# Paired expert rows thinned over the dense phase, their three steps a block apart, the weight split ahead of the dot

## The reference

```python
q = einsum(xb, w_q)                        # 8 heads, 2 halves of 128
s = einsum(q, keys)                        # 128 scores per half
s_top, i_top = top_k(s, 16)                # per half
cand = s_top[0][:, None] + s_top[1][None]  # 256 candidates
best, sel = top_k(cand, 16)
eidx = cand_idx[sel]                       # 16 of 16384 experts per head
gate = softmax(best)
act = gelu(einsum('td,thkd->thk', xb, u_tab[eidx]))
coef = gate * act
h += einsum('thk,thkd->td', coef, v_tab[eidx])
```

## Time and profile before

| | |
|---|---|
| time, median of 3 runs | 2142.16 us (2139.93 to 2144.28) |
| the profiled execution's own time | 2143.07 us |
| its span in the trace | 2141.0 us |
| mean granted TensorE clock | 0.972 of full |
| busy shares | PE 90%, PE weight load 73%, DVE 63%, ACT 29%, POOL 32% |

### The profile page before, as it was taken

One profiled execution on the slowest core, in us unless ns is written; L12 is line 12 of the kernel. 1 busy time (PEld: TensorE's weight loads), 2 busy tenths in 40 slices (PEclk: granted clock), 3 DMA queues, 4 the chain that ended last, 5 costly groups with the idle time before them and its releaser, 6 DMA issues.

```text
span 2141.0 us, 29757 instructions
## 1 busy us (share of the span) xinstructions
PE 1934.9 (90%) x10912; PEld 1564.2 (73%) x10912; DVE 1358.9 (63%) x2860; ACT 616.4 (29%) x1217; POOL 675.5 (32%) x556
## 2 busy tenths in 40 slices
PE   5998889988996988999999999998899998999886
PEld 4997889978966988998999999998544433434332
DVE  3219263353345535488988888988377777776663
ACT  4223312252224324444445444445300000000000
POOL 0003012100000000232333233232277776776663
PEclk9999899988998999999999999999999999999999
DMA  3557158637614573899999999999499999999997
GB/s 117 197 198 220 31 180 260 216 86 257 237 41 178 177 261 119 318 366 349 403 388 361 388 394 357 376 364 376 184 412 403 404 407 412 397 398 415 405 414 290
DMA packets 244650, 629.25 MB, mean 294 GB/s; under 512 B 19714, under 2 KB 137541, under 8 KB 226712
## 3 DMA queue, kind: packets, MB, share of 16 engines
q0 software_dynamic: 74880, 377.52, 44.5%
q1 hardware_dynamic: 169632, 249.92, 34.4%
HBM read 584.36 MB, written 110.21 MB: 324 GB/s over the span
## 4 chain that ended last, share of the span: by engine, by line
DMA 19%; PE 15%; DVE 14%; issue 7%; ACT 2%; POOL 2%; SPq 1%; DVEq 1%; another core or an unknown queue 0%; ACTq 0%; POOLq 0%
DMA ex_w_raw<-in_peer_ut 10%; DMA ex_uv_row<-value_rows,ex_eidx 9%; PE ps L2137 9%; DVE ex_fin L2388 4%; DVE ex_w_lo L1935 3%; POOL ex_uv_row L2066 2%; PE ps L589 2%; PE ps L590 2%; PE ps L591 2%; DVE ex_uv_row L2376 2%; ACT ex_w_hi L2199 1%; DVE ex_q_s L2401 1%; DVE ex_top_i L2335 0%; SPq L1989 0%; DVEq L162 0%
## 5 line engine op out<-in xcount | busy, mean ns | idle before, releaser
L2137 PE MATMUL ps<-ex_uv_row,ex_q_s 128*128 128x512 f32 (+1 forms) x1208 | 542.4, 599 | 61.3 <-DVE ex_q_s L2401 47.3
L2137 PEld LDWEIGHTS ps<-ex_uv_row,ex_q_s 128*128 128x128 f32 (+1 forms) x1208 | 217.1, 187 | 366.3 <-issue 347.6
L2066 POOL DMA_INDIRECT ex_uv_row<-value_rows,ex_eidx x384 | 405.2, 1055 | 214.6 <-issue 102.2
L589 PE MATMUL ps<-x_hi,ex_w_lo 128*128 128x384 f32 (+2 forms) x1296 | 427.6, 330 | 27.8 <-DVE ex_w_lo L1935 22.6
L590 PE MATMUL ps<-x_lo,ex_w_hi 128*128 128x384 f32 (+2 forms) x1296 | 423.6, 327 | 0.0
L591 PE MATMUL ps<-x_hi,ex_w_hi 128*128 128x384 f32 (+2 forms) x1296 | 423.5, 327 | 0.0
L2050 POOL DMA_INDIRECT ex_uv_row<-in_peer_uv,ex_eidx x128 | 190.6, 1489 | 410.2 <-DVE ex_fin L2388 404.7
L2388 DVE SCALAR_TENSOR_TENSOR ex_fin<-ex_uv_row,ret_tables,ex_fin 128x1024 f32<-128x1024 f32 x218 | 278.7, 1279 | 0.3
L589 PEld LDWEIGHTS ps<-x_hi,ex_w_lo 128*128 128x128 f32 x1296 | 244.6, 189 | 40.7 <-DVE ex_w_lo L1935 30.7
L591 PEld LDWEIGHTS ps<-x_hi,ex_w_hi 128*128 128x128 f32 x1296 | 245.0, 189 | 0.0
L590 PEld LDWEIGHTS ps<-x_lo,ex_w_hi 128*128 128x128 f32 x1296 | 244.8, 189 | 0.0
(11 more groups left out here) (415 smaller groups left out, 3418.5 us busy)
## 6 DMA issues: line engine op xcount, KB each, us to landing
value_rows<-in_peer_uv SPq DMA_DIRECT2D x64, 1024.0 KB
ex_w_raw<-in_peer_ut SPq DMA_DIRECT2D x128, 512.0 KB
value_rows<-ex_z_rows SPq DMA_DIRECT2D x128, 128.0 KB
first_raw<-in_w_in SPq DMA_DIRECT2D x8, 1024.0 KB, 7.9
ex_w_raw<-in_peer_wq SPq DMA_DIRECT2D x16, 512.0 KB
value_rows<-ex_z_rows SPq DMA_DIRECT2D x128, 64.0 KB
dp_w_raw<-in_w_in SPq DMA_DIRECT2D x14, 512.0 KB
ex_uv_row<-value_rows,ex_eidx POOLq DMA_INDIRECT x384
```

Of the source, the lines that this page charges most:

```text
L589: pe.matmul(out, left(llo, c), right(rhi, c), start=(c == 0), stop=False)
L2066: pool.indirect_dma_start(value_slot(p)[0], None, k.value_rows, bass.IndirectOffsetOnAxis(ap=eidx[:, u, n % TOPK:n % TOPK + 1], axis=0), e ...
L2137: ins = pe.matmul(k.pv[j % 2][0:r, c, :], spread[:, on_tensor[p] % SPREADS, 0:r], v[:, c * 512:(c + 1) * 512], start=first, stop=last)
```

## The change

Which block a row is taken at now comes from a table, `row_at`: rows begin at block 6 instead of 8, and no row is taken at blocks 16, 32, ... 128. That leaves 130 rows (`beside`) beside the loop; the last six stand behind it. On DVE `lower(i + 2)` comes ahead of `dot`. ACT takes `row` one row later than DVE's `dot`, and the sum (`add_vector`, and `add_row` on PE) two rows later than the dot. The condition in PE's loop asks for a row above 129, which no block has, so all eight sample rows are summed behind PE's loop. Nothing is left out of the computation and the order of the sums is the same.

```diff
-ROWS_FROM = 8
+ROWS_FROM = 6
...
+    row_at = dict(zip((i for i in range(ROWS_FROM, len(blocks)) if i % TOPK), range(PAIRS)))
+    beside = len(row_at)
...   PE
-                    if HK <= i - ROWS_FROM - 1 < PAIRS:
-                        add_row(i - ROWS_FROM - 1)
-                for p in range(len(blocks) - ROWS_FROM - 1, PAIRS):
+                    if row_at.get(i, 0) > HK + 1:
+                        add_row(row_at[i] - 2)
+                for p in range(max(HK, beside - 2), PAIRS):
                     add_row(p)
...   ACT
-                    if 0 <= i - ROWS_FROM < PAIRS:
-                        row(i - ROWS_FROM)
+                    if row_at.get(i, 0) > 0:
+                        row(row_at[i] - 1)
...
-                for p in range(len(blocks) - ROWS_FROM, PAIRS):
+                for p in range(beside - 1, PAIRS):
                     row(p)
...   DVE
-                    p = i - ROWS_FROM
-                    if 0 <= p < PAIRS:
-                        dot(p)
+                    p = row_at.get(i, -1)
                     if 5 <= i + 2 < len(blocks) and by_dve(i + 2):
                         lower(dve, i + 2)
-                    if 0 < p <= HK:
-                        add_vector(p - 1)
-                    if p == HK:
+                    if p >= 0:
+                        dot(p)
+                    if 1 < p <= HK + 1:
+                        add_vector(p - 2)
+                    if p == HK + 1:
                         add(0)
...
-                for p in range(len(blocks) - ROWS_FROM, PAIRS):
+                for p in range(beside, PAIRS):
                     dot(p)
+                    if p <= HK + 1:
+                        add_vector(p - 2)
+                    if p == HK + 1:
+                        add(0)
```

## The result

The changed kernel took 2126.64 us (median of 20 runs, 2122.09 to 2131.91), the kernel before 2141.51 beside it (20 runs, 2124.12 to 2148.48): a ratio of 0.9932, 95% interval 0.9918 to 0.9946. It is faster by 14.9 us, inside the range of 2100 to 2133, and by little more than half of the 27 us forecast. The 95% interval of a ratio is given in brackets from here on. The profiled execution took 2126.57 us, its span is 2124.5.

The account below looks back on a forecast made before the run. PE, DVE and DMA were all near their limit in the dense phase, with some 36 us of PE stalls from late loads. Stalls 20 plus loop end 7 make 27 us off, so 2115 us, range 2100 to 2133.

Parts of the forecast that it names:

- The stalls: Dense phase: of some 36 us of PE stalls, 20 us go, with the loop ending at about 1499.
- the reading: Dense phase: a self-feeding loop, DVE's late dot delaying ACT, the store, the next load and DVE again.
- The wait for the dot: ACT in the dense phase: its wait for DVE's dot falls from 140.8 to under 20 us.
- I count nothing: DVE's order, `lower` ahead of the dot: no gain or loss, since DVE's cycle is the same either way.
- The slower rival: Dot exposed behind DVE's wait for `w_hi`: +37 us, less 20 and 7, about 2152; chance 0.05.
- The rate: DMA in the dense phase: 226.7 MB to move by the loop's end, going above 374 GB/s (378).
- The end of the loop: From PE's last dense block to the first value row: 7 us gained, 5.8 plus 1 for PE's clock.
- Gain 5.8: Loop's end: first value row at 1536.6 instead of 1542.42, before any stall is saved; between 4 and 7.7 us.
- the terms of row 135: Last row behind the loop: gather issued at T + 2.1, landed T + 10, dot ended T + 11.2, value row about T + 17.3.
- The value gathers: Loop's end: last store in at about T + 3.6, value gathers from T + 4, their 6.8 us hidden under sample rows.
- The value phase: After the dense phase: fed by DMA at a share of 1.01, it moves as a whole.
- The limit of bandwidth: HBM at about 358 GB/s per core would need 633 us, leaving a gain near zero; the trace disagreed.

Follow-up runs that it names:

- the stagger alone: Kernel before with only the distances changed: activation one row and sum two rows behind the dot; 0.9932 of the kernel before.
- the thinning alone: Kernel before with only the `row_at` table: rows from block 6, none at blocks 16, 32, ... 128; 0.9921 of the kernel before.
- the order alone: Kernel before with only `lower` put ahead of the dot on DVE; 1.0269 of the kernel before, 57 us slower.
- the kernel without empty blocks and with the dot first: Changed kernel with a row in every block from 6 to 141 and the dot ahead of `lower`; 0.9964 of the kernel before, median 2129.55 us.
- the change with the dot first: Changed kernel with the dot ahead of `lower` again, as in the kernel before; 0.9905 of the kernel before.
- the kernel with small last gathers: Changed kernel with the gathers of rows 133 to 135 fetching 8 floats per partition instead of 2048; 0.9911 of the kernel before.
- the filler: Changed kernel with two unneeded DVE sums over `x_first` added in each of the eight empty blocks; 0.9945 of the kernel before.
- the kernel with rows from block 4: Changed kernel with rows from block 4, dot ahead of `lower`, sample rows 128 and 129 summed in PE's loop; 0.9895 of the kernel before, median 2120.52 us.

## Why the prediction was half right

**The stalls: right in size, the reading borne out in part.** An end of the loop near 1499 was forecast, with 20 us of stalls gone; measured 1500.8 and 17.9. PE's wait for `w_lo` fell from 22.6 to 11.6 us (about 10 forecast). That ACT's wait for the dot delayed the store, and the store the next load, fits the stagger alone, which is 15 us faster. But there PE still waits 16.7 us, and with the thinning alone ACT waits 121.2 us for the dot and PE only 9.8. So this link is one way to the stalls and not the only one. The stagger alone and the thinning alone each bring as much as the whole change (0.9932 and 0.9921 against 0.9932), in their profiles 9 and 16 us of the dense phase, and together 18: for the most part they take away the same stalls.

**The wait for the dot: less than said.** It fell to 44.9 us, not under 20. With the dot ahead of `lower` it is 24.4, in the stagger alone 14.8. The step that failed here is that of `lower`, "I count nothing". The cycle of DVE is indeed the same in either order, but the ring that matters also runs through ACT. The slower rival had the place right (the dot behind the wait for `w_hi`), gave +37 us by DVE's load, and the order alone costs 57 by another mechanism: a ring of 4.44 us at the least and 5.2 or more where DVE has a part of `retrieve`. In the change the stagger opens that ring; by the middles (0.9932 against 0.9905) the order still costs some 6 us there, which the intervals don't set apart from nothing.

**The rate: wrong in sign.** DMA was to go above 374 GB/s; it is 371, with 1.00 for the share. The prediction's bytes had one gather behind the loop's end; three were issued there. So by 1500 the loop had moved 371 x 600 us = 222.6 MB from 900 on, not 226.7, and did not need a faster queue. That a faster one can be had the kernel without empty blocks and with the dot first shows, at 376 GB/s over the same window. That kernel and the change with the dot first (0.9964 and 0.9905) stand apart, so the thinning is worth something beside a stagger from block 6; against the stagger alone (0.9932) that is not shown. In three of the changed kernel's units of 16 blocks, 48 to 96, block to block takes 70.89 us, which is 14 x 4.21 and 2 x 5.78 within 0.4: hardly a stall is left there. What remains stands mostly at both ends of the phase, and the two largest stalls lie behind the loads that SP issues after its series of small DMAs.

**The end of the loop: the step that failed by size and sign.** "Gain 5.8", plus 1 for the clock: 7. Measured: T to V grew by 12.3 us, all that the six moved rows had freed, and V to the end by 1.9; the gain is -2. The error is in the terms of row 135. Its gather was issued at T + 5.1, not T + 2.1: PE began row 128, whose slot it needs, only at T + 1.6, since ACT formed that row's factors late, behind the `z_rows` of block 142 (1501.04), and when PE was done at T + 3.5, POOL was still at the issue of row 134's gather, until T + 4.8. Then 11.1 us passed from issue to dot, not 7.9. Together that is 6.2 us, and V came at T + 23.3 instead of T + 17.3. From the dot on the chain was right: 7.1 us measured, 7.3 forecast. The value gathers went wrong as well: the first started at T + 17.1, not T + 4, because the store ahead of it took 13.7 us and was in at T + 16.3, where the sum had it in at T + 3.6. But it had landed (1522.32) 1.3 us before DVE was free for the first `picked` (1523.60), so this second error lay beside the first and not on top of it. That the kernel with small last gathers has V at T + 16.8, close to the 17.3 of the prediction, is in part luck: its row 135 was issued late too and landed in time because it was small. The steps named were the true ones; what was missing is the price of three gathers, the last store and POOL's own issues at the same time.

That the total came out inside the range is owed to the stalls. Of 27 us, 20 were to come from them and 18 did; 7 were to come from the end and 2 were lost there.

**The value phase**: 598 to 601 us in every kernel, so it moves as a whole, as said.

**The limit of bandwidth.** The Trainium skill (DMA: Bandwidth & Descriptors, Specifications) gives 358 GB/s for one core, and works it out as half of 716 for two cores. The changed kernel, one core alone, ran at 371 over 600 us and 405 over 570 us, so that half is no ceiling for it, and the measurement decides again.

**Open.** Whether the order of `lower` costs anything in the full change (0.9932 and 0.9941 against 0.9905) is not settled, nor whether the filler costs the last few us, nor whether an empty block helps by its missing gather or by ACT's free time. No run moved SP's two series of small DMAs, and none shortened the last gathers alone or the last store alone. Which of the store's companions delays it most, the three gathers or the 512 KB load of the norm's weights between the stores (10.1 us to landing, 3.7 before), was not tried apart.

## What to carry to other kernels

When an engine waits inside its own queue, write the order of each engine out as one ring and add up a turn: a ring through two engines that both have idle time can be slower than the engine that you look at, and a step back by one block opens it. Add up the longest turn too: a ring without reserve passes on every extra piece of work. When two edits remove the same stall, do not add them; take each alone. And work that is moved out of a loop must be priced with the transfers it then runs beside. List every path that the next phase waits for (here the last gather by way of dot and norm, and the last store by way of the first value gather), and check in the trace which one ended last: the engine that starts without idle time is on it.

## What the hardware did that I had not expected

The last store of `z_rows`, 64 KB, took 13.7 us beside three gathers of 1 MB, 7.3 in the kernel with rows from block 4, 5.1 beside the small gathers, and 1.8 in the kernel before, where no gather ran. Over 4 us the hardware queue, which has the stores and the norm's weights, moved 181 packets of some 2 KB beside 146 of the gathers' 7.5 KB, and 720 of 1.3 KB beside the small gathers. The queue of smaller packets got a quarter of the bytes. The Trainium skill (DMA: Bandwidth & Descriptors, Queues, rings and completion order) says that each engine takes turns between the queues at the grain of a packet; the packet counts of the two queues, 181 and 146 where the sizes are 2 and 7.5 KB, agree with it as far as they go: the shares are nearer to even by packets than by bytes. Whether the profile counts as a packet what that page calls one, no run here shows.

Second, the issue of an indirect gather on POOL was not of one price. In the kernel before, 80 of the 136 gathers of pairs took POOL about 1.7 us and 33 about 0.9; in the changed kernel 28 and 85. Row 135's took 1.06 before and 1.99 in the changed kernel. What sets it was not looked into.
